# State-space groups of a one-core transformer block: one memory for both stages of a group, work moved between the stages, and token work moved between engines

## The reference, cut to what matters

```python
q = partial_rope(rms_norm(q.reshape(bsz, s, ATT_HEADS, ATT_HEAD_DIM), q_norm_g[l]), cos_a, sin_a)
k = partial_rope(rms_norm(k.reshape(bsz, s, ATT_KV_HEADS, ATT_HEAD_DIM), k_norm_g[l]), cos_a, sin_a)
...
xbc = jax.nn.silu(causal_depthwise_conv(xbc, conv_w[l], conv_b[l]))
xs, bm, cm = jnp.split(xbc, [SSM_D_INNER, SSM_D_INNER + SSM_GROUPS * SSM_STATE], axis=-1)
dt = jax.nn.softplus(dt_raw.astype(f32) + dt_bias[l].astype(f32))
y = ssd(xs, dt, a, bm, cm)                      # chunked scan, 128 tokens to a chunk
y = y + d_skip[l].astype(f32)[:, None] * xs
y = y * jax.nn.silu(z_ssm)
y = rms_norm(y by group, ssm_norm_g_2)
y_ssm = y @ w_branch_ssm[l]
```

## Time and profile before

| | us |
|---|---|
| median of 3 runs | 2991.51 (2989.92 to 2991.55) |
| the profiled execution, its own time | 2986.61 |
| its span | 2984.8 |
| PE busy in the span | 2587.9 (87%) |
| token stage, first PE transpose to last | 1159.4 to 1388.1 |
| state-space branch, first PE product to last | 1974.3 to 2870.7 |

### The profile page before, as it was taken

The page is one execution under the profiler, slowest core; times in us unless marked ns, Lnnn a source line. Parts: engine busy times, 40 slices in busy tenths (PEclk is TensorE's granted clock), DMA queues, the critical chain, the costliest instruction groups (busy, mean ns, idle before and its releaser), DMA issues. The chain is left out here.

```text
span 2984.8 us, 40399 instructions
## 1 busy us (share of the span) xinstructions
PE 2587.9 (87%) x15847; PEld 1414.9 (47%) x15847; DVE 1663.8 (56%) x2973; ACT 899.1 (30%) x1334; POOL 562.5 (19%) x492
## 2 busy tenths in 40 slices
PE   5999683989799995887999799989899899899878
PEld 3555342545355552443444477435545545545533
DVE  5885875222133226783999866434734734834843
ACT  5110502112122223333522255223523513513510
POOL 1111032000000002443421000002402402402413
PEclk8999795999899997998999899999999999999999
DMA  8553859699999994210022100421011011010042
GB/s 228 195 186 105 335 181 358 223 377 375 381 360 370 372 333 170 75 36 29 29 78 99 50 1 1 149 92 36 1 64 36 1 64 36 1 64 29 1 185 97
DMA packets 185104, 433.08 MB, mean 145 GB/s; under 512 B 26416, under 2 KB 35888, under 8 KB 184816
## 3 DMA queue, kind: packets, MB, share of 16 engines
q1 hardware_dynamic: 158112, 365.39, 34.3%
q0 software_dynamic: 10176, 32.78, 3.5%
q10 hardware_dynamic: 16656, 32.66, 3.1%
HBM read 371.85 MB, written 58.93 MB: 144 GB/s over the span
## 5 line engine op out<-in xcount | busy, mean ns | idle before, releaser
L1245 PE MATMUL m_gu<-conv_y,m_xT 128*64 128x256 f32 x1024 | 234.3, 388 | 21.3 <-DMA arena<-in_moe_w_up 19.1
L1247 PE MATMUL m_gu<-arena,m_xT 128*64 128x256 f32 x1024 | 234.3, 388 | 0.0
L1323 DVE TENSOR_TENSOR m_hid<-m_sg,m_gu 64x256 f32<-64x256 f32 x96 | 39.6, 413 | 339.7 <-ACT m_sg L1293 339.7
L2496 POOL TENSOR_TENSOR y_A<-steps,consts 128x1024 f32<-128x1024 f32 x32 | 64.5, 2014 | 848.6 <-POOLq L2280 697.8
L1247 PEld LDWEIGHTS m_gu<-arena,m_xT 128*64 128x64 f32 x1024 | 143.3, 140 | 73.7 <-issue 15.4
L1267 PE MATMUL m_y_ps<-arena,m_hidT 128*64 128x512 f32 x768 | 175.4, 598 | 0.0
L140 PE MATMUL i_pj<-hT,i_ws 128*128 128x512 f16 x384 | 149.4, 389 | 22.7 <-DVE i_ws L410 22.7
L1245 PEld LDWEIGHTS m_gu<-conv_y,m_xT 128*64 128x64 f32 x1024 | 143.4, 141 | 39.7 <-issue 29.0
L141 PE MATMUL i_pj<-hT,i_ws 128*128 128x512 f16 x384 | 149.2, 389 | 0.0
L142 PE MATMUL i_pj<-hT,i_ws 128*128 128x512 f16 x384 | 149.0, 388 | 0.0
L141 PE MATMUL s_pj<-hT,arena 128*128 128x512 f16 x384 | 148.0, 385 | 0.0
(11 more groups left out here) (504 smaller groups left out, 6422.5 us busy)
## 6 DMA issues: line engine op xcount, KB each, us to landing
arena<-in_moe_w_down SPq DMA_DIRECT2D x32, 2048.0 KB, 21.8
arena<-in_moe_w_up SPq DMA_DIRECT2D x22, 2048.0 KB, 24.7
conv_y<-in_moe_w_gate SPq DMA_DIRECT2D x22, 2048.0 KB, 20.7
hT<-in_moe_w_gate SPq DMA_DIRECT2D x10, 2048.0 KB, 20.9
hT<-in_moe_w_up SPq DMA_DIRECT2D x10, 2048.0 KB, 23.4
conv_y<-in_ada_w SPq DMA_DIRECT2D x8, 2048.0 KB, 7.9
x_tok<-in_ada_w ACTq DMA_DIRECT2D x6, 2048.0 KB, 12.7
slot_out<-m_y ACTq DMA_DIRECT2D x96, 128.0 KB, 6.2
```

What stands on the lines that cost most here:

```text
L1245: g = nc.tensor.matmul(gu_ps[i][g_rows, 0:FFN // 2], lhsT=xT[:, c, :], rhs=k.wg[e % WEIGHT_SLOTS][:, c, cols], start=c == 0, stop=c == KC - 1)
L1247: u = nc.tensor.matmul(gu_ps[i][u_rows, 0:FFN // 2], lhsT=xT[:, c, :], rhs=k.wu[e % WEIGHT_SLOTS][:, c, cols], start=c == 0, stop=c == KC - 1)
L1323: nc.vector.tensor_tensor(hid[:, i, :], sg[:, i, :], gu_ps[i][u_rows, 0:FFN // 2], ALU.mult) \
L2496: nc.gpsimd.tensor_tensor(A[:, s], per_head(k.adt, t, P), k.const("after").unsqueeze(1).to_broadcast([P, HPG, P]), ALU.mult) \
```

## The change

- `EARLY_Z` is 2 instead of 4: two z tiles of each group move from the input stage to iterations 4 and 5 of the scan.
- `alloc_group_views`: the working tiles of both stages lie in one block of memory (`group_words`) instead of each stage having its own, so that a stage can leave data for the next. The z weights are loaded into `yT`, the branch weights into memory of their own.
- POOL makes A and the values of chunks 0 and 1 at the end of the input stage (`segment_operand`, `chunk_values`); in the scan it begins at chunk 2.
- The pairs of the branch weights are made in the input stage (`split_branch`, one of 128x1024 on ACT and on DVE for each of j = 2 to 5); both loads of 2 MB are issued behind tile 2.
- Tile 0 of the next group's weights is split at the end of the scan (ACT behind its last transposed chunk, DVE behind branch product 11), so that in groups 1 to 3 the first matmul waits for no pair.
- The branch products use six banks; product 4 and 5 take the banks of the state products. The last chunk's state is not made any more (PE, DVE).
- Token stage: gain and shift of the turned tile are made by ACT (8 activations with scale and bias, in `high_tokens`, behind three evacuations in the loop) instead of DVE; the ten heads are scaled by ACT (10 activations of 128x128 with a scale) instead of one DVE instruction; the gain vector is multiplied by DVE (two instructions) instead of POOL. `normalise(t+3)` stands behind the small key work in DVE's order.

```diff
-EARLY_Z = 4
+EARLY_Z = 2
...
             def high_tokens(t):
+                act.wait_ge(h_turned, t + 1)
+                if t:
+                    act.wait_ge(h_low, t)
+                for c in range(KC):
+                    last = nc.scalar.activation(full[:, c, :], tp[:, c // 4, (c % 4) * P:(c % 4 + 1) * P], ACT.Identity,
+                                                scale=gain[:, c:c + 1], bias=shift[:, c:c + 1])
+                last.then_inc(h_full, 1)
...
                 nc.scalar.activation(ss[:, t % 2], ss[:, t % 2], ACT.Sqrt).then_inc(std, 1)
+                act.wait_ge(inverse, t + 1)
+                for h in range(QK_HEADS):
+                    x = raw[:, t % 2, h * HD:(h + 1) * HD]
+                    last = nc.scalar.activation(x, x, ACT.Copy, scale=ss[:, t % 2, h:h + 1])
+                last.then_inc(scaled, 1)
...
-                pool.wait_ge(scaled, t + 1)
-                by_head = qk.rearrange("p (h d) -> p h d", d=HD)
-                for n, (a, b) in enumerate(((0, HEADS), (HEADS, QK_HEADS))):
-                    nc.gpsimd.tensor_tensor(by_head[:, a:b, :], by_head[:, a:b, :],
...
-                v.tensor_tensor(heads, heads, ss[:, s, 0:10].unsqueeze(2).to_broadcast([P, QK_HEADS, HD]),
-                                ALU.mult).then_inc(scaled, 1)
-                if t + 3 < TT:
-                    normalise(t + 3)
+                v.reciprocal(ss[:, s], ss[:, s]).then_inc(inverse, 1)
...
-                dve.wait_ge(gained, 2 * t + 2)
+                if t + 3 < TT:
+                    normalise(t + 3)
+                dve.wait_ge(scaled, t + 1)
+                for n, (a, b) in enumerate(((0, HEADS), (HEADS, QK_HEADS))):
+                    last = v.tensor_tensor(heads[:, a:b, :], heads[:, a:b, :],
+                                           gq[:, n, :].unsqueeze(1).to_broadcast([P, b - a, HD]), ALU.mult)
+                    step(last)
...
+def alloc_group_views(k, ctx):
+    words = k.sb("group_words", [P, 9 * D], ctx=ctx)
...
+    k.y_A = at(0, 2 * D).rearrange("p (a h l) -> p a h l", a=2, l=P)
...
+def segment_operand(k, g, t):
+    heads = slice(g * HPG, (g + 1) * HPG)
+    return k.nc.gpsimd.tensor_tensor(k.y_A[:, t % 2], k.adt[:, t, heads].unsqueeze(2).to_broadcast([P, HPG, P]),
+                                     k.const("after").unsqueeze(1).to_broadcast([P, HPG, P]), ALU.mult)
...
+def chunk_values(k, g, t):
...
+    return (tt(k.y_xdt[:, t % 2], xs, per_head(k.dt[:, t, heads]), ALU.mult),
+            tt(k.y_xds[:, t % 2], xs, per_head(k.e_after[:, t, heads]), ALU.mult),
+            tt(k.y_xd[:, t % 2], xs, per_head(k.d_skip[:, heads]), ALU.mult))
...
+        @block.gpsimd
+        def _(pool):
+            pool.wait_ge(low, splits(4))
+            pool.wait_ge(pj_done, 5)
+            for t in range(2):
+                segment_operand(k, g, t).then_inc(pool_done, 1)
+            pool.wait_ge(low, splits(5))
+            pool.wait_ge(tr_done, 8)
+            pool.wait_ge(tr_out, 8)
+            for t in range(2):
+                for last in chunk_values(k, g, t):
+                    last.then_inc(pool_done, 1)
...
             for j in range(6):
-                pe.wait_ge(high, j + 1)
-                pe.wait_ge(low, j + 1)
+                if splits(j):
+                    pe.wait_ge(high, splits(j))
+                    pe.wait_ge(low, splits(j))
...
                 if j + 1 < 6:
                     split(j + 1)
+                if j >= 2:
+                    split_branch(j - 2)
...
-        ring = [br[:, :], seg[:, 0:HALF], seg[:, HALF:S], yd_ps[:, :]]
-        bank = lambda j: ring[0] if j < KC else ring[(j - KC) % 4]
+        ring = [br[:, :], yo_ps[:, :], st_ps[:, :], seg[:, 0:HALF], seg[:, HALF:S], yd_ps[:, :]]
+        bank_of = [0, 0, 0, 0, 1, 2, 0, 1, 2, 3, 4, 5, 0, 1, 2, 3]
+        bank = lambda j: ring[bank_of[j]]
...
-                if t == TT - EARLY_Z:
-                    act.wait_ge(k.w_branch_in, 16)
-                    for c in range(4):
-                        nc.scalar.activation(ws[:, 0, c], w[:, c], ACT.Copy, scale=gain[:, c:c + 1]) \
-                            .then_inc(q["w_high"], 1)
+            if g + 1 < SSM_GROUPS:
+                act.wait_ge(next_in, 16)
+                act.wait_ge(q["seg_done"], TT - 1)
+                high_part(nc, k.first_ws[:, 0], k.w_first[:, :, :]).then_inc(q["f_high"], 1)
...
-                if TT - EARLY_Z <= t < TT - EARLY_Z + 2:
-                    for c in range(2 * (t - TT + EARLY_Z), 2 * (t - TT + EARLY_Z) + 2):
-                        dve.wait_ge(q["w_high"], c + 1)
-                        v.scalar_tensor_tensor(ws[:, 1, c], in0=w[:, c], scalar=gain[:, c:c + 1], in1=ws[:, 0, c],
-                                               op0=ALU.mult, op1=ALU.subtract).then_inc(q["w_low"], 1)
```

More of the change, by code:

```diff
@@ L1705, in normalise @@
                 v.tensor_scalar(k.x_tok[:, t, :], row0[:, s], rstd[:, s, 1:2], None, ALU.mult).then_inc(normed, 1)
[L1707 to L1714, removed]
             def angles():
@@ L2335, in _ @@
                     for c in range(KC):
-                        last = product(nc, pj[j % 2][:, a:a + HALF], part(ws, j % 2, c),
+                        last = product(nc, pj[j % 2][:, a:a + HALF], part(ws[j % 2], c),
                                        part(k.hT, c, slice(a, a + HALF)), c == 0, c == KC - 1)
@@ L2361, in split, with split_branch @@
             def split(j):
-                dve.wait_ge(high, j + 1)
-                low_part(nc, ws[:, 1, j % 2].rearrange("p c q -> p (c q)"), raw(j).rearrange("p c q -> p (c q)"),
-                         ws[:, 0, j % 2].rearrange("p c q -> p (c q)")).then_inc(low, 1)
-            split(0)
+                dve.wait_ge(high, splits(j))
+                low_part(nc, ws[j % 2][:, 1].rearrange("p c q -> p (c q)"), raw(j).rearrange("p c q -> p (c q)"),
+                         ws[j % 2][:, 0].rearrange("p c q -> p (c q)")).then_inc(low, 1)
+            def split_branch(c):
+                dve.wait_ge(b_high, c + 1)
+                v.scalar_tensor_tensor(k.ws_branch[:, 1, c], in0=k.w_branch[:, (c + 1) * D:(c + 2) * D],
+                                       scalar=gain[:, c:c + 1], in1=k.ws_branch[:, 0, c],
+                                       op0=ALU.mult, op1=ALU.subtract).then_inc(b_low, 1)
+            if g == 0:
+                split(0)
+            v.tensor_scalar(gain[:, :], k.pv("ssm_norm_g_2", 4 * g, 4), W_UP, None, ALU.mult).then_inc(gained, 1)
+            dve.wait_ge(gained, 1)
             for j, tile in enumerate(tiles):
@@ L2393, in split, with split_branch @@
                     act.wait_ge(pj_done, j - 1)
-                high_part(nc, ws[:, 0, j % 2], raw(j)).then_inc(high, 1)
+                high_part(nc, ws[j % 2][:, 0], raw(j)).then_inc(high, 1)
+            def split_branch(c):
+                if c == 0:
+                    act.wait_ge(wb_in, 16)
+                    act.wait_ge(gained, 1)
+                else:
+                    act.wait_ge(b_low, c)
+                nc.scalar.activation(k.ws_branch[:, 0, c], k.w_branch[:, (c + 1) * D:(c + 2) * D], ACT.Copy,
+                                     scale=gain[:, c:c + 1]).then_inc(b_high, 1)
             def activate(j):
@@ L2612, in _ @@
             decay(0)
[L2613 removed]
+            act.wait_ge(q["small"], 1)
             for t in range(TT + 2):
@@ L2640, in _ @@
             v.memset(eps[:, :], EPS).then_inc(q["small"], 1)
-            v.tensor_scalar(gain[:, :], k.pv("ssm_norm_g_2", 4 * g, 4), W_UP, None, ALU.mult).then_inc(q["small"], 1)
-            dve.wait_ge(q["small"], 2)
+            dve.wait_ge(q["small"], 1)
             def decayed(t):
```

149 lines of the change are left out of this document (81 added, 68 removed).

## The result

The changed kernel takes 2863.89 us (median of three executions, 2858.64 to 2864.43; a fourth of 4550.52 us, at a granted clock of 0.55, is left out), against 2991.53 us before: ratio 0.9569, 95% interval 0.9552 to 0.9586. A second timing gave 0.9564 (0.9550 to 0.9579). The forecast was 2881, range 2866 to 2907: right in sign, and in the branch right in mechanism, but 17 us too high, and the result lies 2 us under the range.

The account below looks back on a forecast made before the run. PE, busy 87% of the span, was taken as the bound, with 93.9 us of waits in the branch. 2986.6 less 105.7 (branch) and 4.5 (token stage) gives 2876.4; 4.9 from profile to median makes 2881, range 2866 to 2907.

Parts of the forecast that it names:

- "issue" wait: Before the first branch product, PE waits for DVE's last branch-weight pairs: 19.8 us in 4 waits, forecast to go.
- one wait for exp: Scan's second wait, for A(1), becomes one for ACT's exp of chunk 0: 0.75 us kept, gain 2.8.
- the starts stayed warm: Rival: group start and hand-over stay at 1.2 GHz though waits shrink; 14.0 us back, 2895; chance 0.12.
- the hand-over is neither POOL's nor DVE's: Rival, input stage to scan: values and convolution interleave badly, PE waits 2 to 4 us a group, 2893; chance 0.10.
- iterations 6 and 7: Rival: scan finds another bound there, DVE adding two branch products beside its chunk; 2909; chance 0.04.
- the 2 MB load delays no evacuation: Rival, input stage: ACT waits for the loads at `split_branch(0)`, tile 2's evacuation queued behind; 2992 and up; chance 0.02.
- put down to the clock, for 29.6: Branch: half clock behind removed waits goes; 7.2 us at group starts, 6.8 in first segments, 15.6 around iteration 6.
- cover and pairs: Scan iterations 4 and 5: z products cover them, branch pairs leave; 41.4 us of waits and 15.6 of clock.
- 3.2, ready at 6.1, a gain of 1.1: Token tile: ACT's eight gain-and-shift pieces take 3.2 us, ready 6.1 after the turn instead of 7.2.
- Even: Token tile: ten scales take ACT 3.0 us for DVE's 1.49, but `normalise` falls from 2.86 to about 0.9.
- The rival in which ACT lengthens the tile: Token stage: each engine's added time counts, 2.0 us x 8 tiles, +16 instead of -4.5; 2902; chance 0.09.
- the token stage's bound of -17: Lower bound of the token term: 0.2 us an ACT instruction, down to PE's own work.

Follow-up runs that it names:

- both corners of the square: Changed kernel with the turn's gain and shift back on DVE: 2866.08 us; with head scales back on DVE and head gains on POOL: 2868.08 us.

## Why the prediction was 17 us too high

In the branch what it named came about, or nearly: no "issue" wait, one wait for exp of 0.89 (0.7 to 0.8 said), 0.9 us of waits for DVE's additions (none said), group period 195.7 to 197.9 (197 to 199), full clock in the windows, hand-over under 2 us. The token period didn't: 23.65 us for the 25.4 it named. None of the rivals came about: the starts stayed warm, the hand-over is neither POOL's nor DVE's, iterations 6 and 7 have waits of 0.22 us, and the 2 MB load delays no evacuation.

**The branch, 105.7 for 112.6.** The waits gone are 71.5 us, forecast 72.7 with the transposes; the last chunk's state is 3.4 by the same row. The term left out is the overlap: 32 waits fewer at 0.165 us are 5.3 us. The remainder, 32.4 us, is put down to the clock, for 29.6. Read place by place in the two traces, with the waits taken out, the clock gives 7.3 us at the starts of groups 1 to 3, 7.6 in the first two iterations and 18.4 around iteration 6 (for 7.2, 6.8 and 15.6): 33.3, within 0.9 of the remainder. By part, undoing gave 63.9 for 57.0 (cover and pairs with their clock), 20.0 for 17.1, 15.7 for 14.7, 15.8 for 12.5. They come to 115.4, more than the 109.2 that 112.6 leaves beside the last chunk's state. Of the excess 1.7 us are the cold start of group 2 with the chunks in the scan; the rest may be that cover and pairs, back in another order, cost more than they did before, which wasn't tried. Nor was the last chunk's state by itself.

**The token stage, 4.5 for 14.2.** This is the step that failed: a steady tile was to lose 1.1 us and lost 2.88. Along the chain the 2.88 are 1.81 from turn to cast, 0.81 in POOL's fetch and 0.28 at `normalise` (2.90, 0.02 too much by rounding). "3.2, ready at 6.1, a gain of 1.1" had ACT start 0.34 us too late (behind the residual the evacuations took 1.38, not 1.7) and gave the eight pieces 0.28 too much (2.92): 1.8 for 1.1. POOL's fetch behind DVE's additions (0.8) was in no term. "Even" for the scales looked at whether DVE is free sooner, and was near for the end of `normalise` (0.28), but not at what else they move: by themselves they take the index key's steps out of the chain (1.45 a tile in all), and behind the turn's move they free the low half (0.68). By tiles: -8.6 for -3.3 on tiles 4 to 6, +0.1 for +2.3 on the first, -5.7 for -3.5 on tile 7 and the tail. The rival in which ACT lengthens the tile is refuted by both corners of the square.

The sizes on ACT themselves were near. Eight pieces took 2.92 us and ten scales 3.03, for 3.2 and 3.0. The Trainium skill, "ScalarE: Activation LUTs", section "What ACT_TABLE_LOAD costs", had given 3.1 and 2.9; the trace agrees within 0.2. Its rule that plain adds and multiplies belong on VectorE (section "Rules for kernel authors") would have made the tile longer; in this stage both moves to ScalarE shorten it, because the chain waits for the engine's order and not for the instruction's length.

**From profile to median, 4.9.** The profiled execution of before lay 4.9 us under its median, the changed kernel's 0.5 over its own. That was a property of the one execution, and adding it was no mistake: the median of before in four later timings is 2989.6 to 2991.1, and the stretches that the change doesn't touch came to 1857.6 us in that profile, for 1857.1 to 1864.1 and a median of 1861.0 in the 17 traces here. The changed kernel's profile has 1861.9 there, which is the 4.3 us that the table seems to lose. Both sides nearly cancel, and the sum closes: 9.7 + 6.9 + 4.9 - 4.3 = 17.2 of 17.1. So 16.6 of the 17 us are the two stages' own.

The range's low end went down by the whole 12.5 us to the token stage's bound of -17, but by 2 only for everything else; the branch alone was worth 6.9 more. The waits of the earlier trace rows could be counted, what each hides could not from that view.

## What to carry to other kernels

When work moves to another engine, write out the old engine's order after the move before pricing the moved instructions: the steps that come ahead or fall out of the chain were worth more here than the instructions. Price a removed wait as the wait, the clock behind it where the rows show it low, and the overlap of neighbours that it had broken. Two moves on one chain can share their gain: each alone was worth 1.45 and 2.20 us, both 2.88. The token tile went from 26.5 to 23.65 us by the moves, and from there to PE's own 21.45 by order alone.

## What the runs showed of the hardware

- A wait in PE's rows costs 0.165 us more than it says, where its neighbours would overlap (five waits of 3.16 us made a group 4.00 us longer).
- DVE and POOL slow each other in single instructions, the issue of an indirect DMA too: 0.98 us alone, 1.79 beside a DVE addition of 1024 columns; the squares of 1280 columns 2.33 and 3.39; the addition itself 1.28 and 3.13 to 3.23.
- The clock behind the same wait differed. In the run with chunks 0 and 1 in the scan, 2.87 or 2.88 us without work left the next 16 segments at half clock in one group (3.78 us, and 3.75 for the next 16), for the most part in two (3.14 and 3.43), and not at all in one (2.05). Waits of 0.94 and 0.89 left it full in all. Behind 2.1 to 2.3 us at a group's start it was full in most, and low in two (2.12 and 2.24).
